# RWKV preparation of the main stream in one stage, with the low-rank columns projected first

## What is computed

```python
def rwkv_branch(cols, s0, mu, w0, w2, a0, a2, g2, k_k, k_a, r_k, lnx_g, lnx_b):
    cols = cols + (bidir_shift(cols) - cols) * mu
    r, k, v, w_lo, a_lo, g_lo = jnp.split(cols, ...)      # 512, 512, 512, 128, 128, 128 columns
    w_log = -jax.nn.softplus(-(w0 + jnp.einsum('bldr,drc->bldc', jnp.tanh(w_lo), w2))) - 0.5
    decay = jnp.exp(-jnp.exp(w_log))                      # per direction d
    iclr = jax.nn.sigmoid(a0 + jnp.einsum('bldr,drc->bldc', a_lo, a2))
    kk = l2norm(heads(k * k_k))
    k_dir = heads(k[:, :, None, :] * (1 + (iclr - 1) * k_a))
    b_dir = kk[:, :, None] * heads(iclr)
    y, s_fin = rwkv7_scan(both_dirs(r_h), per_dir(decay), per_dir(k_dir), both_dirs(v_h), both_dirs(-kk), per_dir(b_dir), s0)
    ...
    bonus = jnp.einsum('blhn,bldhn,hn->blh', r_h, k_dir, r_k)[..., None] * v_h
    y = (y + bonus) * gate
```

## Time and profile before

| | us |
|---|---|
| median of 3 runs | 3184.2 (3179.57 to 3186.72) |
| profiled execution | 3184.11 |
| its span, first to last instruction | 3182.3 |
| TensorE busy in the span | 2621.7 (82%) |
| VectorE busy | 921.6 (29%) |
| ScalarE busy | 414.1 (13%) |

### The profile page before, as it was taken

One profiled execution on the slowest core, in us unless ns is written; L12 is line 12 of the kernel. 1 busy time (PEld: TensorE's weight loads), 2 busy tenths in 40 slices (PEclk: granted clock), 3 DMA queues, 4 the chain that ended last, 5 costly groups with the idle time before them and its releaser, 6 DMA issues. The chain is left out here.

```text
span 3182.3 us, 43968 instructions
## 1 busy us (share of the span) xinstructions
PE 2621.7 (82%) x19719; PEld 1413.1 (44%) x19719; DVE 921.6 (29%) x1897; ACT 414.1 (13%) x808; POOL 85.3 (3%) x93
## 2 busy tenths in 40 slices
PE   7969569999999889898899899675673786969995
PEld 4534234324433334434344333264561785745553
DVE  0227443002212122312122211245545443043222
ACT  1131011100110000111111201120112221000001
POOL 0010000000000000000000000000000110000000
PEclk9978668999999999899999999887885897979998
DMA  5308037998899988898889888540000003259996
GB/s 178 119 27 286 6 123 298 375 391 336 348 398 379 367 358 343 358 375 351 347 330 378 362 355 366 227 159 1 1 20 7 3 3 122 93 197 406 422 422 282
DMA packets 158869, 789.18 MB, mean 248 GB/s; under 512 B 18241, under 2 KB 20553, under 8 KB 110937
## 3 DMA queue, kind: packets, MB, share of 16 engines
q1 hardware_dynamic: 155225, 773.78, 61.3%
q0 software_dynamic: 3456, 12.58, 1.0%
HBM read 774.79 MB, written 11.53 MB: 247 GB/s over the span
## 5 line engine op out<-in xcount | busy, mean ns | idle before, releaser
L2998 PE MATMUL bank<-ring,arena 128*34 128x512 f32 (+1 forms) x3072 | 710.9, 606 | 76.6 <-DMA ring<-in_w_up 62.3
L2998 PEld LDWEIGHTS bank<-ring,arena 128*34 128x34 f32 x3072 | 180.2, 118 | 496.2 <-issue 470.7
L3022 PE MATMUL bank<-ring,arena 128*34 128x512 f32 x1408 | 320.2, 597 | 46.9 <-DMA ring<-in_w_down 46.2
L3022 PEld LDWEIGHTS bank<-ring,arena 128*34 128x34 f32 x1408 | 79.1, 112 | 278.2 <-issue 152.4
L303 PE MATMUL bank<-arena,ring 128*128 128x256 f32 (+1 forms) x688 | 158.8, 394 | 11.3 <-DMA ring<-in_w_in 9.7
L303 PEld LDWEIGHTS bank<-arena,ring 128*128 128x128 f32 x688 | 134.3, 196 | 36.1 <-issue 10.5
L3459 PE MATMUL bank<-ring,arena 128*64 128x256 f32 x992 | 111.3, 379 | 4.2 <-DMA ring<-in_moe_w_up 3.4
L2898 PEld LDWEIGHTS bank<-arena 64*64 64x64 f32 x2304 | 75.4, 139 | 54.6 <-issue 54.2
L313 PE MATMUL bank<-ring,arena 128*128 128x512 f32 (+1 forms) x224 | 98.8, 596 | 0.0
L3459 PEld LDWEIGHTS bank<-ring,arena 128*64 128x64 f32 x992 | 73.3, 137 | 45.8 <-issue 13.9
L3010 PEld LDWEIGHTS bank<-consts,arena 34*128 34x128 f32 x704 | 82.4, 191 | 14.9 <-issue 14.1
(11 more groups left out here) (633 smaller groups left out, 3079.8 us busy)
## 6 DMA issues: line engine op xcount, KB each, us to landing
ring<-in_w_gate SPq DMA_DIRECT2D x128, 1408.0 KB, 9.0
ring<-in_w_up SPq DMA_DIRECT2D x128, 1408.0 KB, 12.2
ring<-in_w_down SPq DMA_DIRECT2D x176, 1024.0 KB, 8.4
ring<-in_w_in SPq DMA_DIRECT2D x46, 1024.0 KB, 6.4
ring<-in_moe_w_down SPq DMA_DIRECT2D x33, 1024.0 KB, 15.5
ring<-in_moe_w_gate SPq DMA_DIRECT2D x31, 1024.0 KB, 14.1
ring<-in_moe_w_up SPq DMA_DIRECT2D x31, 1024.0 KB, 17.3
ring<-in_ada_w SPq DMA_DIRECT2D x24, 1024.0 KB, 6.9
```

The costliest lines, as they stand in the source:

```text
L2998: last = mm(ps[c][row:row + CAP, 0:n], xsT[:, e, k, :], w[:, at:at + n], start=k == 0, stop=k == KT - 1)
L3022: last = mm(ps[6][row:row + CAP, :], hidT[:, 2 * j + f, :], w[:, f, half * BANK:(half + 1) * BANK], start=j + f == 0, stop=j == FT // 2 - ...
```

## The change

The three phases become one. The low-rank columns are projected first, then k; then come the low-rank products of both directions, then r, then v. A bank now holds a tile's decay product in its first half and its iclr product in the second, so a direction needs four banks, and r's projection waits only for direction 0's sigmoids, v's for direction 1's. `cs7`, `e7` and `t7` exist twice and lie in the arena; nothing shares the place of `w2sb` and `a2sb`, which SP fetches at the end of the stage before, ahead of the two pieces of v.

VectorE mixes a whole group with two wide operations and one more for each tile, waiting between them but not between tiles. Between k and r it works both directions' scans, subtracts the middle of each chunk, asks for the exponentials and forms the keys. The bonus uses the sum of both directions' keys once (`rk7`), and ScalarE copies it; v is turned by half-width matmuls straight into two partition halves, and ScalarE copies that too. The roots, reciprocals and last products follow v's mix. The end phases `N_PHASES_R`, `N_PHASES_R2` are renumbered accordingly. The scans and all behind them are as before.

```diff
@@ SP
-            issue(n_rwkv - 8, n_rwkv)
+            issue(n_rwkv - 8, n_rwkv - 2)
             sp.wait_ge(phase_ended, 4 * N_PHASES_R)
             for dst, src in ((w2sb, A["rwkv_w2_2"]), (a2sb, A["rwkv_a2_2"])):
                 sp.dma_start(dst, src.rearrange("d r c -> (d r) c")).then_inc(w2_landed, up(w2_landed, 16))
+            issue(n_rwkv - 2, n_rwkv)
@@ ScalarE
+            shifted_act(0)
             act.wait_ge(lo_asked, due(act, lo_asked))
-            ACTV(wl, wl, ACT.Tanh).then_inc(act_order, up(act_order))
-            act.wait_ge(act_order, own(act, act_order))
-            ACTV(gl, gl, ACT.Sigmoid).then_inc(lo_ready, up(lo_ready))
...
+            ACTV(wl, wl, ACT.Tanh).then_inc(lo_ready, up(lo_ready))
+            ACTV(gl, gl, ACT.Sigmoid)
+            shifted_act(1)
             for d in range(2):
                 act.wait_ge(zw_ready, due(act, zw_ready))
...
+            for n in (2, 3):
+                shifted_act(n)
+            for n in range(2):
+                act.wait_ge(sum7_ready, due(act, sum7_ready))
+                ACTV(t7[n], ps[n][:, :], ACT.Sqrt, bias=eps_col).then_inc(root7, up(root7))
+            for d in range(2):
                 act.wait_ge(e7_asked, due(act, e7_asked))
...
+            act.wait_ge(bonus7_ready, due(act, bonus7_ready))
+            for n in range(2):
+                ACTV(flat4(bonus[:, 2 * n:2 * n + 2, :]), ps[2 + n][:, :], ACT.Copy)
+            for c in range(NCL):
+                act.wait_ge(v7_filled, due(act, v7_filled))
+                ACTV(v7[:, c].rearrange("p q v -> p (q v)"), ps[4 + c][:, 0:SEQ], ACT.Copy)
@@ VectorE
+            def mixed7_dve(n, dsts, first):
...
+                dve.wait_ge(shift_ready, due(dve, shift_ready))
+                settled(TT(mix7[:, 0:w, :], x[:, 0:w, 0:SEQ], x[:, 0:w, 2:2 + SEQ], ALU.add))
+                settled(STT(mix7[:, 0:w, :], mix7[:, 0:w, :], 0.5, x[:, 0:w, 1:1 + SEQ], ALU.mult, ALU.subtract))
+                for ct, dst in enumerate(dsts):
+                    last = STT(dst, mix7[:, ct, :], pc("rwkv_mu_2", first + ct), x[:, ct, 1:1 + SEQ], ALU.mult, ALU.add)
+                last.then_inc(shift_read, up(shift_read))
...
             for d in range(2):
                 dve.wait_ge(sig_ready, due(dve, sig_ready))
...
+                settled(TT(chunks(cs7[d]), chunks(cs7[d]), middles(dmid[d]), ALU.subtract))
+                TT(dboth[d], dend[d], dmid[d], ALU.subtract)
+                settled(TT(al7[d], cs7[d], al7[d], ALU.subtract))
+                dve.drain().then_inc(e7_asked, up(e7_asked))
                 for q in range(4):
+                    last = TS(kt7[d][:, q, :], bt7[d][:, q, :], 1.0, pc("rwkv_k_a_2", q), ALU.subtract, ALU.mult)
+                settled(last)
+                settled(STT(flat4(kt7[d]), flat4(kt7[d]), 1.0, flat4(k7), ALU.add, ALU.mult))
+            mixed7_dve(2, [r7[:, ct, :] for ct in range(4)], 0)
+            settled(TT(rk7, kt7[0], kt7[1], ALU.add))
+            for q in range(4):
+                last = STT(rk7[:, q, :], r7[:, q, :], pc("rwkv_r_k_2", q), rk7[:, q, :], ALU.mult, ALU.mult)
+            last.then_inc(k7_ready, up(k7_ready))
+            mixed7_dve(3, [vT7[:, ct, :] for ct in range(4)], 8)
+            for n in range(2):
+                dve.wait_ge(root7, due(dve, root7))
+                settled(nc.vector.reciprocal(t7[n], t7[n]))
+                settled(TT(two(n), two(n), t7[n], ALU.mult))
+            for d in range(2):
+                settled(TT(bt7[d], bt7[d], kk7, ALU.mult))
+            for d in range(2):
                 dve.wait_ge(e7_ready, due(dve, e7_ready))
+                TT(al7[d], al7[d], kk7, ALU.mult)
+                TT(bt7[d], bt7[d], e7[d], ALU.mult)
+                TT(kt7[d], kt7[d], e7[d], ALU.mult)
+                settled(TT(rt7[d], rt7[d], r7, ALU.mult))
@@ TensorE
+            by_feature(pe, 0, rwkv_pieces[0], u2x_lat, SEQ)
+            by_feature(pe, 4, rwkv_pieces[1], u2x_lat, SEQ)
+            pe.wait_ge(w2_landed, due(pe, w2_landed, 32))
+            pe.wait_ge(lo_ready, due(pe, lo_ready))
+            lows_pe(0)
             pe.wait_ge(shift_ready, due(pe, shift_ready, 2))
+            lows_pe(1)
+            pe.wait_ge(sig_ready, due(pe, sig_ready))
+            by_feature(pe, 0, rwkv_pieces[2], u2x_lat, SEQ)
+            pe.wait_ge(sig_ready, due(pe, sig_ready))
+            by_feature(pe, 4, rwkv_pieces[3], u2x_lat, SEQ)
...
+            for n in range(2):
+                last = mm(ps[2 + n][:, :], C["half_ones"], flat4(rk7[:, 2 * n:2 * n + 2, :]), start=True, stop=True)
+            last.then_inc(bonus7_ready, up(bonus7_ready))
+            pe.wait_ge(shift_ready, due(pe, shift_ready))
+            pe.wait_ge(shift_read, due(pe, shift_read, 2 + 4))
             for c in range(NCL):
                 for q in range(4):
-                    last = mm(ps[c][0:C7, q * P:(q + 1) * P], vT7[:, q, c * C7:(c + 1) * C7], ident, start=True, stop=True)
+                    for h in range(2):
+                        r = half7(h)
+                        last = mm(ps[4 + c][r, q * C7:(q + 1) * C7], vT7[:, q, c * C7:(c + 1) * C7], ident[:, r], start=True, stop=True)
```

More of the change, by code:

```diff
@@ L622, in build @@
         w2sb, a2sb = ar(512), ar(512)
+        cs7, e7 = ([by_pair(SEQ) for _ in range(2)] for _ in range(2))
+        rk7, mix7 = by_pair(SEQ), by_pair(SEQ)
+        t7 = [ar(TOKS2) for _ in range(2)]
+        SP2 = SEQ + 2
+        shift_in = [ar(4 * SP2, "p (c t) -> p c t", c=4) for _ in range(2)]
         spare = [0]
@@ L641, in build @@
         id7 = flat7[:, 16 * C7:17 * C7]
[L643 to L647, removed]
+        rwkv_pieces = [column_pieces(A["w_in_2"], 2064 + g * 512, n) for g, n in ((3, 384), (1, 512), (0, 512), (2, 512))]
         n_rwkv = len(pieces)
@@ L2140, in _ @@
                 dve.wait_ge(signal, own(dve, signal))
-            for n in range(4):
-                dve.wait_ge(shift_ready, due(dve, shift_ready))
[L2143 to L2157, removed]
+            ones64 = C["ones"][:, 0:C7]
@@ L2158, in _ @@
+            mixed7_dve(0, (wl, al, gl), 12)
             dve.drain().then_inc(lo_asked, up(lo_asked))
+            mixed7_dve(1, [k7[:, ct, :] for ct in range(4)], 4)
             for q in range(4):
                 last = TS(kk7[:, q, :], k7[:, q, :], pc("rwkv_k_k_2", q), None, ALU.mult)
-            last.then_inc(dve_order, up(dve_order))
-            dve.wait_ge(dve_order, own(dve, dve_order))
+            settled(last)
+            two = lambda n: kk7[:, 2 * n:2 * n + 2, :].rearrange("p q t -> p (q t)")
@@ L2183, in _ @@
-            dve.drain().then_inc(phase_ended, 1)
-            dve.wait_ge(phase_ended, phase_end(dve))
-            ones64 = C["ones"][:, 0:C7]
+                TT(t7[n], two(n), two(n), ALU.mult).then_inc(k7_ready, up(k7_ready))
             for d in range(2):
@@ L2327, in _ @@
                 dve.wait_ge(dve_order, own(dve, dve_order))
-                TT(bonus[:, q, :], bonus[:, q, :], vlat7[:, q, :], ALU.mult).then_inc(dve_order, up(dve_order))
+                TT(bonus[:, q, :], bonus[:, q, :], vT7[:, q, :], ALU.mult).then_inc(dve_order, up(dve_order))
                 dve.wait_ge(dve_order, own(dve, dve_order))
@@ L3200, in _, with lows_pe @@
             pe.wait_ge(phase_ended, phase_end(pe))
-            for n in range(4):
-                base = 4 * (n % 2)
-                if n >= 2:
-                    pe.wait_ge(shift_ready, due(pe, shift_ready))
-                by_feature(pe, base, rwkv_pieces[n], u2x_lat, SEQ)
-            pe.wait_ge(shift_ready, due(pe, shift_ready, 2))
+            def lows_pe(d):
+                ks = slice(64 * d, 64 * d + 64)
+                for q in range(4):
+                    mm(ps[4 * d + q][:, 0:SEQ], w2sb[ks, q * P:(q + 1) * P], wl[ks, :], start=True, stop=True)
+                    last = mm(ps[4 * d + q][:, SEQ:2 * SEQ], a2sb[ks, q * P:(q + 1) * P], al[ks, :], start=True, stop=True)
+                last.then_inc(zw_ready, up(zw_ready))
@@ L3217, in _ @@
             pe.wait_ge(phase_ended, phase_end(pe))
-            def decays_pe(d):
-                ks = slice(64 * d, 64 * d + 64)
-                if d == 0:
-                    pe.wait_ge(w2_landed, due(pe, w2_landed, 32))
-                    pe.wait_ge(lo_ready, due(pe, lo_ready))
-                for q in range(4):
-                    mm(ps[q][:, 0:SEQ], w2sb[ks, q * P:(q + 1) * P], wl[ks, :], start=True, stop=True)
-                    last = mm(ps[4 + q][:, 0:SEQ], a2sb[ks, q * P:(q + 1) * P], al[ks, :], start=True, stop=True)
-                last.then_inc(zw_ready, up(zw_ready))
-                for q in range(4):
-                    pe.wait_ge(k7_ready, due(pe, k7_ready))
-                    mm(ps[q][:, 0:SEQ], C["half_ones"], e7[:, q, 0:SEQ], start=True, stop=True).then_inc(bonus7_ready, up(bonus7_ready))
-                pe.drain().then_inc(phase_ended, 1)
-                pe.wait_ge(phase_ended, phase_end(pe))
             def products7_pe(n):
@@ L3305, in level7_pe @@
```

(2 more changed lines are left out.)

116 lines of the change are left out of this document (29 added, 87 removed).

## The result

The changed kernel took 3099.57 us (median of 4 runs, 3092.36 to 3105.22), the kernel before beside it 3181.89 us (4 runs, 3172.09 to 3186.72). The ratio is 0.9744, with an interval of 0.9712 to 0.9775: faster. The forecast was 3106.2 us in a range of 3099 to 3114, so the median lies only 0.6 us above the lower bound. The profiled execution took 3092.36 us, with a span of 3090.6 us and a mean granted clock of 0.902 (before: 3182.3 us, 0.887).

The account below looks back on a forecast made before the run. The order of a serial chain was taken to bound the stage. TensorE until v, v's copy and VectorE's 24.2 us tail put the first product at 2394.1 instead of 2472.0: 3184.1 - 77.9 = 3106.2 us, range 3099 to 3114.

Parts of the forecast that it names:

- What bounds the stage: RWKV preparation of the main stream: only the order of a serial chain bounds it; TensorE idle 77.6 of 166 us.
- TensorE until v: TensorE from first projection to v's end: 54.06 us projections, 7.2 us low-rank matmuls and 0.3 us of waits.
- the two waits: TensorE's waits for the sigmoids, direction 0's before r's projection, direction 1's before v's: 0.3 us for both.
- VectorE's front: VectorE's work from k's mix to the bonus product: done before v is copied, with 3.0 us of slack.
- The tail: VectorE's work after v is copied (mix, reciprocals, products) up to the scans' first product: 24.2 us.
- the eight products: VectorE's last 1024-column products of both directions, unwaited: 1.13 us a step, 9.3 us in all, upper bound 10.1 us.
- The stage: First projection to the scans' first product: 87 to 89 us, which takes 77.9 us off.
- The distance from the first product to the end: From the scans' first product to the kernel's end: unchanged, all that follows shifts as a whole.
- The clock rival: Clock falls in TensorE's low-rank matmuls and r's projection starts cold: 6.0 us more, 3112.2 us; chance 0.12.
- the slower rival: Granted clock stays at 0.50 beyond the stage: 3195 us with 30 us of full-rate work in the scans; chance 0.03.
- The rival without VectorE's overlap: Unwaited VectorE operations don't overlap and its front part becomes late: 2.8 us more, 3109.0 us; chance 0.06.
- the wait of 6.99 us: TensorE's wait in the kernel before for late-issued w2 and a2: claimed to go with their earlier issue.

Follow-up runs that it names:

- e3_serial: Changed kernel's instructions with the interleaving taken out, projections first and the rest one after the other: 3111.64 us, ratio 0.9784 to the kernel before, stage 100.89 us.
- e7_tail3: Changed kernel with three added 1024-column additions on VectorE right behind v's mix: 3098.13 us, stage 91.31 us, one execution.
- e9_lows6: Changed kernel with each direction's low-rank products done six times over: stage 121.57 us, one execution.
- e8_waited: Changed kernel with VectorE's scans, mixes, scalings and products in the stage each waiting for the one before: stage 91.52 us, one execution.
- e10_w2early: Kernel before with only w2 and a2 fetched earlier, ahead of the last two pieces: 3177.35 us, ratio 0.9983 to the kernel before, stage 163.31 us.
- e2: Kernel before measured again, unchanged, under a new label: ratio 0.9998 to the kernel before, stage 166.76 us.
- e1: Changed kernel measured again, unchanged: 3102.18 us against 3180.24 us of the kernel before (15 runs), ratio 0.9761, stage 88.21 us.

## Why the prediction was right

- **What bounds the stage** (the order of a serial chain): right. Its part that counts is not the overlap but the length of the chain, as e3_serial shows. The prediction never split the two, since it added up the new chain from its parts; a reader who credited the gain to interleaving would have been wrong by 65 us of 78.
- **TensorE until v**: 61.5 us forecast, 61.1 measured (2295.96 to 2357.05). One of the two waits cost 0.42 us, the other doesn't show; 0.3 was said for both. The low-rank products ran at the full clock, as chosen, and took 6.4 us (2322.32 to 2328.74) where the sum had 7.2.
- **VectorE's front**: slack 3.0 us forecast, 3.90 measured. The scans took 3.02 us for sixteen, not 3.4.
- **The tail**: 24.2 us forecast, 24.3 measured (2359.13 to 2383.39), and e7_tail3 shows that it is all on the path. The step of the eight products was 1.13 us, read from operations of 256 columns; it is 1.14 at 1024. Roots and exponentials were ready, and nothing in the eight products waits for ScalarE.
- **The stage**: 88.0 us forecast, 87.53 and 88.21 measured. The saving in the stage is 78.4 us (78.6 with the slower start on both sides), where 77.9 was said. **The distance from the first product to the end** stayed: 710.3 us before, 709.2 in its second profile, 707.1 and 709.6 after.
- **The clock rival** (0.12) is ruled out by the windows above and by e9_lows6, and with it the slower rival, which needed 1.2 GHz for longer.
- **The rival without VectorE's overlap** (0.06) didn't come about: the eight products stepped by 1.14 us. It was priced at 2.8 us; e8_waited measures 3.3. Two errors stand in that price, of opposite sign. The slack was 3.9 us and not 3.0, which makes the 2.8 a 1.9, and each operation loses more than the 0.1 us that I took: 5.16 - 3.02 is 0.13 for each scan.
- **One reason was wrong**, though it carried no number of the sum. The prediction says that the wait of 6.99 us goes with the earlier issue of w2 and a2. By itself that is worth 3.5 us (e10_w2early against e2). The full sum held because the new chain was added up from its own parts, and the phase end and the eight copies of v are not in it.
- **The absolute time**: 3106.2 us was made from a profiled execution of before at 3184.1 us. The difference, 77.9 us, is met by e1 (78.06), but its interval spans 72 to 80 us, so the agreement to 0.2 us is chance; the stage is the sharper test. The absolute numbers are 4 to 7 us lower, since before itself had medians of 3180 to 3183 us in the later measurements and the first four runs of the changed kernel lay low. That the first median stayed inside the range, by 0.6 us, is luck too.

## What to carry to other kernels

Where engines take turns in the slices of a stage, write down the new chain from end to end and price that; the waits that disappear don't add up, since one often covers another. Before you interleave, make the chain shorter: wide operations, one phase, no wait for each tile gave 65 of 78 us here, the overlap on top of them 13. Then ask which engine is last, measure its slack with a few added operations, and move work off its tail.

## What I had not expected of the hardware

- A granted clock of 1.00 held through 41 us of matmuls on 64 of 128 rows (e9_lows6). Eight of the same, in the kernel before, ran all their 7.16 us at 0.50 after an idle time, and so did 12 us of them in e3_serial, both directions in a row. TensorE in e3_serial, the first of them and two windows, of the first projections and of these products:

```profile
2360.88 1.19 PE L3182 MATMUL bank<-arena 64*128 64x256 f32 x2 [3.04 <-ACT arena L1302]
```
```profile
2305.00:2310.00 5.00, 5.00 (x22) 0.89 0.00 0
2361.00:2373.00 12.00, 12.00 (x32) 0.50 0.00 0
```

  So half-height work kept a high clock, but twelve busy us of it didn't raise a low one, where the full-height projections of the same kernel had risen from 0.50 to a mean of 0.89 between 3 and 8 us after their start. Whether half-height work alone would ever raise the clock isn't shown, and neither is which idle time lowers it: e3's products followed one of 3.04 us and ran at 0.50, while the turn of v in the changed kernel followed one of 2.99 us and ran at 1.00:

```profile
2363.40:2366.00 2.60, 2.09 (x64) 1.00 0.03 6
```
- Where the low-rank products change direction, eight matmul instructions pass in the time of four. In the changed kernel:

```profile
2325.02 0.70 PE L3182 MATMUL bank<-arena 64*128 64x256 f32 x4
2325.45 0.70 PE L3183 MATMUL bank<-arena 64*128 64x256 f32 x4
2325.99 0.59 PE L3182 MATMUL bank<-arena 64*128 64x256 f32 x2
```

  Eight instructions start within 0.97 us, where two take 0.43 elsewhere. Direction 0 uses rows 0 to 63 and direction 1 rows 64 to 127, so the last of one seem to run beside the first of the other. To alternate the directions tile by tile could shorten the 6.4 us, and v would come sooner; no run tries it.
- A wait between neighbours on VectorE costs 0.12 to 0.14 us in every size compared (e8_waited against the changed kernel), from 64-column scans to 1024-column products.
- The stage of streamed weights took 1564.4 and 1554.4 us in two executions of code that is the same there. One profiled span doesn't tell two kernels apart to better than about 10 us; the length of a stage without such a stream does, to 0.8 us.
